# Forget-gate page attention: the decays of the second head pair in another quarter of the rows, both pairs' decay products issued together

## The reference, cut to what matters

```python
def fox_attention(q, q_pos, k, v, logf):          # 16 query heads, 4 key heads of 64, float32
    c = jnp.cumsum(logf.astype(F32), axis=1)      # the decay: one running sum per head
    ...
        s = jnp.einsum('bqgrd,blgd->bqgrl', qg, kf) + (c_q - c_k[:, None])
        p, _ = masked_softmax(s, ...)
        return (jnp.einsum('bqgrl,blgd->bqgrd', p, vf).reshape(B, Q, H, D),)
```

## Time and profile before

| what | value |
|---|---|
| median of 3 timed runs | 3932.85 us (3925.16 to 3936.61) |
| the profiled execution, its own time | 3914.76 us |
| its span in the profile | 3913.0 us |
| mean granted TensorE clock | 0.911 |
| TensorE busy (matmul) | 3284.0 us, 84% |
| VectorE, ScalarE, GpSimd busy | 1510.2, 1004.6, 580.5 us |
| the main loop of this stage | from 3208.46 to about 3722 us of the span |

### The profile page before, as it was taken

The page is one execution under the profiler, slowest core; times in us unless marked ns, Lnnn a source line. Parts: engine busy times, 40 slices in busy tenths (PEclk is TensorE's granted clock), DMA queues, the critical chain, the costliest instruction groups (busy, mean ns, idle before and its releaser), DMA issues. The chain is left out here.

```text
span 3913.0 us, 68173 instructions
## 1 busy us (share of the span) xinstructions
PE 3284.0 (84%) x22697; PEld 2138.5 (55%) x22697; DVE 1510.2 (39%) x4439; ACT 1004.6 (26%) x2522; POOL 580.5 (15%) x927
## 2 busy tenths in 40 slices
PE   6899997999998988986547758999588858888869
PEld 5444447888887555653425433665555534444433
DVE  0311112444442355552226555211266635555523
ACT  0100001232321466661103211000155513333311
POOL 0000002222220000001035522000011122222200
PEclk9999997999999599996759969999699969999979
DMA  1455455444441222243458844321622058888632
GB/s 32 165 182 205 172 182 145 126 124 121 124 123 36 74 69 58 66 96 116 185 154 282 280 168 149 107 69 37 200 75 77 24 154 265 266 269 270 217 146 81
DMA packets 341885, 556.92 MB, mean 142 GB/s; under 512 B 74003, under 2 KB 225083, under 8 KB 337899
## 3 DMA queue, kind: packets, MB, share of 16 engines
q1 hardware_dynamic: 265924, 355.43, 29.2%
q0 software_dynamic: 52288, 166.16, 13.3%
q10 hardware_dynamic: 23340, 30.98, 2.3%
HBM read 490.66 MB, written 118.25 MB: 156 GB/s over the span
## 5 line engine op out<-in xcount | busy, mean ns | idle before, releaser
L965 PE MATMUL PS<-cmp_xT,cmp_w 128*128 128x255 f32 (+2 forms) x2176 | 488.5, 375 | 1.1 <-DVEq L1044 1.1
L313 PE MATMUL PS<-even_w,even_xT 128*128 128x512 f32 (+1 forms) x1152 | 476.0, 574 | 1.9 <-DMA even_w<-in_w_in_e 1.9
L965 PEld LDWEIGHTS PS<-cmp_xT,cmp_w 128*128 128x128 f32 x2176 | 395.0, 192 | 47.6 <-issue 1.2
L855 ACT ACTIVATE cmp_xT<-PS 64x512 f32<-64x512 f32 x260 | 155.0, 596 | 870.4 <-PE PS L936 868.9
L313 PEld LDWEIGHTS PS<-even_w,even_xT 128*128 128x128 f32 x1152 | 218.5, 191 | 248.5 <-issue 242.7
L855 DVE COPY cmp_xT<-PS 64x512 f32<-64x512 f32 x260 | 179.3, 690 | 297.0 <-PE PS L936 295.0
L313 PE MATMUL PS<-odd_w,odd_xT 128*128 128x368 f32 x896 | 283.0, 477 | 1.4 <-DVE odd_xT L266 1.4
L1833 PE MATMUL PS<-ident,s_fox_kv 128*128 128x128 f32 x1024 | 180.3, 290 | 65.2 <-ACT s_fox_kT L1787 48.4
L313 PEld LDWEIGHTS PS<-odd_w,odd_xT 128*128 128x128 f32 x896 | 170.4, 192 | 107.1 <-issue 4.0
L873 POOL DMA_DIRECT2D cmp_pairs<-in_cache_nsa x256 | 151.7, 600 | 393.2 <-issue 384.3
L273 DVE COPY even_o<-PS 128x512 f32<-128x512 f32 (+3 forms) x81 | 50.4, 622 | 389.5 <-PE PS L313 379.0
(11 more groups left out here) (436 smaller groups left out, 4838.8 us busy)
## 6 DMA issues: line engine op xcount, KB each, us to landing
s_fox_kv<-in_cache_fox POOLq DMA_DIRECT2D x256, 256.0 KB, 4.8
s_fox_kv<-in_cache_fox SPq DMA_DIRECT2D x256, 256.0 KB, 4.8
cmp_pairs<-in_cache_nsa POOLq DMA_DIRECT2D x256, 128.0 KB, 2.9
cmp_pairs<-in_cache_nsa SPq DMA_DIRECT2D x256, 128.0 KB, 2.8
s_sel_kv<-in_cache_nsa POOLq DMA_DIRECT2D x256, 128.0 KB, 5.0
s_sel_kv<-in_cache_nsa SPq DMA_DIRECT2D x256, 128.0 KB, 5.1
out_dil_sample<-in_cache_dil_w SPq DMA_DIRECT2D x8, 4088.0 KB, 23.9
even_w<-in_w_in_e SPq DMA_DIRECT2D x8, 2048.0 KB, 8.1
```

What stands on the lines that cost most here:

```text
L313: last = nc.tensor.matmul(bank(c, t, 128)[:, 0:n], xT[:, k, t * 128:t * 128 + 128], w[:, c % WS, k, 0:n], start=(k == 0), stop=(k == KT - 1))
L855: last = nc.vector.tensor_copy(dst, x) if l else nc.scalar.activation(dst, x, ACT.Copy)
L965: last = nc.tensor.matmul(hidden_ps(x, NK)[:, g], w1[:, kv, c, :], xT[:, u % 2, kv, g, c % 8, at:at + NK], start=(c == 0), stop=(c == 15))
```

## The change

The decays are now kept twice, once for each pair: pair `p` finds those of tile `j` in row quarter `(j + p) % 4`. The tile is twice as large, and each sequence is loaded with 8 transfers where there were 4. In a round the eight score products of both pairs come first, and after them the eight decay products, tile by tile, each time pair 0 and then pair 1. The column quarter and the PSUM bank of each product are what they were. `scored` goes up after the last decay product of each pair, which are now the seventh and the eighth of the eight.

```diff
-            dec = sb("dec", [128, 2, RB, KW])
+            dec = sb("dec", [128, 2, P, RB, KW])
...
+        def decay_rows(p, j):
+
+            return 32 * ((j + p) % 4)
+
         def load_decay(eng, b):
             if b >= 2:
                 eng.wait_ge(scored, RB * P * (b - 1))
             v = E.decay[b].rearrange("h (k j n) -> j h k n", k=RB, j=4)
-            for j in range(4):
-                eng.dma_start(dec[32 * j:32 * j + 16, b % 2], v[j]).then_inc(dec_in[b % 2], 16)
+            for p in range(P):
+                for j in range(4):
+                    at = decay_rows(p, j)
+                    eng.dma_start(dec[at:at + 16, b % 2, p], v[j]).then_inc(dec_in[b % 2], 16)
...
                     if fox and r % RB == 0:
-                        hold(dec_in[b % 2], 64 * (b // 2 + 1))
+                        hold(dec_in[b % 2], 64 * P * (b // 2 + 1))
                     for p in range(P):
                         x = r * P + p
                         hold(expd if fox else s_free, x - 1)
                         for j in range(4):
                             last = nc.tensor.matmul(PS[32 * j:32 * j + 32, s_bank(x)], q[:, p, b, :], kT[:, p, j, :], start=True, stop=not fox)
-                        if fox:
-                            for j in range(4):
-                                rows = slice(32 * j, 32 * j + 16)
-                                last = nc.tensor.matmul(PS[32 * j:32 * j + 32, s_bank(x)], hsel[rows, p, :], dec[rows, b % 2, r % RB, :], start=False, stop=True)
-                        last.then_inc(scored, 1)
+                        if not fox:
+                            last.then_inc(scored, 1)
+                    if fox:
+                        for j in range(4):
+                            for p in range(P):
+                                rows = slice(decay_rows(p, j), decay_rows(p, j) + 16)
+                                last = nc.tensor.matmul(PS[32 * j:32 * j + 32, s_bank(r * P + p)], hsel[rows, p, :], dec[rows, b % 2, p, r % RB, :], start=False, stop=True)
+                                if j == 3:
+                                    last.then_inc(scored, 1)
```

## The result

The changed kernel takes 3942.97 us (median of 20 runs, 3927.57 to 3956.05), the kernel before 3922.81 (20 runs, 3906.96 to 3936.61). The ratio is 1.0054, with a 95% interval of 1.0041 to 1.0066: slower by some 20 us, where a change of -1.3 us, too small to measure, was forecast.

A forecast was written before the change was run, and what follows sets the result against it. Rounds were taken to hang on TensorE, then VectorE, then TensorE again. Rounds -4.9, first two rounds -1.4 and opening +5.0 gave -1.3 us: 3913.5 profiled, 3931.5 on the median; range 3922 to 3942, 8 in 10 3914 to 3950.

The forecast's parts named there:

- The link on VectorE: In ordinary rounds, VectorE's two maxima and key copy hold their times, so TensorE's 0.70 us saving becomes waiting.
- rival (b): In each round the eight decay products don't run together; up to 1.0 us more a round, about 3990 us; chance 0.08.
- The 0.41 for a pass of 512 columns: On TensorE, time of one product pass alone, used to argue that row parts in different banks run at once.
- A round gains 0.08: Main loop: each of 61 rounds gets 0.08 us shorter (0.0 to 0.15), 4.9 us in all.
- I take 5.0: Opening: eight more decay transfers ahead of the first key loads on SyncE's queue cost 5.0 us (2.7 to 5.5).
- In the main loop ... this is hidden: Main loop: extra decay transfers cost SyncE 2.8 us a sequence, covered by keys asked for six rounds ahead.
- Rival (c), the clock: Main loop: TensorE, less densely at work, falls to half clock more often; around 3945 us; chance 0.12.

The follow-up runs named there:

- e4: Changed kernel, with VectorE copying tile 0's turned keys between pair 0's and pair 1's maxima instead of after both; ratio 0.9977 to the kernel before.
- e3: Changed kernel with only a pair's own 8 heads in each copy of the decays: still eight transfers, bytes as before; ratio 1.0070 to the kernel before.
- e7: Changed kernel without the decay loads of sequences 2 to 7, which reuse the decays of sequences 0 and 1; ratio 1.0030 to the kernel before.
- e12: Kernel before without the decay loads of sequences 2 to 7, which reuse the decays of sequences 0 and 1; ratio 1.0000.
- e1: Kernel before, in its old product order, with every decay transfer made twice and only the first copy used; ratio 1.0029.
- e5: Changed kernel with each sequence's eight main-loop decay transfers spread 3, 3 and 2 ahead of three key loads; ratio 1.0054 to the kernel before.
- e6: Changed kernel with the eight decay transfers of sequence 1 moved from the opening to behind the barrier; ratio 1.0047 to the kernel before.

## Why the prediction was wrong, step by step

- **"The link on VectorE"** was right, in its mechanism and nearly in its numbers: maxima at 1.84 and 2.52 (forecast 1.80 and 2.49), copy at 3.15 (3.12), transposes of pair 1 at 3.71 (3.68), all eight decay products together (rival (b) fell). e4 confirms it from the other side. (The 0.41 for a pass of 512 columns was a little low: the row mixes in passes of 280 columns, 21 in 192. Nothing hangs on it.)
- **"A round gains 0.08"**, 4.9 us in all, did not come. The best rounds went from 7.133 to 7.094, half of that; the 55 rounds without stops (those within 0.5 us of before, the first two left out) came to +0.5 us together. The first two rounds gave 1.6 us (forecast 1.4).
- **"I take 5.0" for the opening** failed: it measured 10.5. I had put the cost between issue time (5.5) and bytes (2.7), as if one or the other counted. Both stretches of the opening grew, one behind the other. SyncE's time from its first decay transfer to its first key load grew by 4.2 (9.74 to 13.99), and from there to the barrier by 6.2 (26.60 to 32.82). In that second stretch the DMA engines were full before and after (share 1.04 and 1.05), but moved 292 GB/s instead of 349: the small packets of the decays share them with GpSimd's key loads. 1183 of them still had to go in that stretch, against 345 before. The records of the whole opening say the same: 1024 more packets of 1 KB at 79 ns are 5.1 us on 16 engines, and the 1536 packets of 4 KB took 270 ns instead of 214, another 5.4. e3 shows that bytes alone are the small part: with no byte more than before, its two stretches are 13.90 and 30.44 us, and the rate in the second is 305 GB/s. Why the same bytes move more slowly there is open.
- **"In the main loop ... this is hidden"** failed, and is the second half of the loss: the term of the loop's loads was put at nothing and measured 14.6 us (521.6 against e7's 506.9). No key came late, which is what I had looked at; but the transfers compete with a reader that no line of the kernel issues, the fetch of TensorE's own instructions. Without the loads the new order's loop is 3.1 us shorter than the old one's; with them it is 10.4 longer. The loss sits in few rounds: 27, 33, 34, 36, 51 and 52 make 12.7 of the 14.6 us between e7 and the changed kernel.
- **Rival (c), the clock.** The measured 3943 us is close to its price (3945) by luck: that price was 12 us above a median of three runs, 3932.85, and twenty runs have put that median at 3922.81. By the same luck the time lies inside the 8-in-10 range (3914 to 3950), while the difference, 20 us, is far beyond what the sum's own bounds allow (4.1 us with no gain in the rounds and 5.5 for the opening). Half-clock time in the loop did go from 24.7 to 34.6 us, with four falls more, in rounds 27, 33, 51 and 52. It was not the thinner work of ordinary rounds that brought them: e7 has the same rounds and 10.8 us. In rounds 27 and 33 the fall comes within 1.0 us of the end of a stop (3447.37 and 3501.98), so there it follows the stop; for the others that is argued, and e7 has two falls, in rounds 19 and 20, with no stop.

What stays open: why fetches start later with the new order, 4.9 against 3.5 us in the median, even without decay loads (e7 and e12). That the new order simply uses up its instructions sooner is not it in the changed kernel: 256 records take 9.5 us ahead of the stop of round 27, as in e1. It plays a part in e4, where they take 8.8. Open too is why e5, e6 and e7 are 0.2% slower in timed runs than opening and loop of their one profile say. Their profiled executions are 11, 4 and 7 us faster than the medians of their runs, so part of it is which execution was profiled; the stops differ from one to the next. The split of the 20 us into opening and loop rests on single executions in the same way.

## What to carry to other kernels

Before a reordering is priced on the engine that it relieves, ask which engine's program order stands next, and change that order in the same edit: here one moved copy on VectorE turned +0.54% into -0.23%, and with two edits to the loads into -0.63%. Extra transfers ahead of a barrier cost more here than either their issue time or their bytes: 10.5 us where the two alone were put at 5.5 and 2.7, since the full DMA engines also moved the loads behind them more slowly. In a long unrolled stage look for "issue" waits inside groups of TensorE. If they stand a multiple of 256 TensorE records apart, they are waits for instructions, and a burst of small transfers just ahead can lengthen them. Leaving the loads out gave some 9 us back in timed runs (e7); spreading them did not show there (e5).

## What the runs showed of the hardware

- TensorE stops in the middle of a group, for 0.7 to 3.9 us, always behind record 256n + 192 of its program, give or take one (23 of 23 stops), and goes on 2.4 to 3.3 us after the start of an instruction fetch of 16 KB. 198 such fetches serve its 50759 records. Fetches are about 10 us apart in the loop, and 10.4 to 17.0 before stops.
- In the loop the fetch of a packet starts once TensorE has come to within 1.4 us of the position before: in the median 3.5 us after it in the kernel before, and up to 12.7 us after it in the changed one.
- Eight products in four row quarters, four column quarters and two banks start within 0.05 us of one another (3408.042 to 3408.089) and have their second passes 0.24 later: as quick as four.
- With full DMA engines 8 more transfers of 128 KB in packets of 1 KB cut what is moved from 349 to 292 GB/s.
